# A fused fp32 model on one core: two homes for the scan's decay rows, another order inside a scan tile, and the weights' low parts written over their raw copies

## What is computed

```python
def hybrid_mixer(h, pos, w_in, conv_w, conv_b, ...):
    ...
    xs, b_in, c_in = split_cols(xbc, (SSD_INNER, SSD_GROUPS * SSD_STATE, SSD_GROUPS * SSD_STATE))
    ...
    dtf = jax.nn.softplus((dt_f + dt_bias_f).astype(jnp.float32)).reshape(b, s, SSD_GROUPS, SSD_HPG)
    ...
    y_fwd = ssd_chunked(xh, dtf, af, b_in, c_in)
    ...
    y = y_fwd + y_bwd + d_skip.reshape(SSD_GROUPS, SSD_HPG, 1).astype(xh.dtype) * xh
    y = gated_group_rmsnorm(y.reshape(b, s, SSD_INNER), z, ssd_norm_g)
    branch_ssd = y @ w_br_ssd
    ...
    return (g_ssd * branch_ssd + g_attn * branch_attn) @ w_out
```

## Time and profile before

| what | value |
|---|---|
| three runs | 2862.0, 2860.92, 2841.12 us |
| their median | 2860.92 us |
| the profiled execution | 2826.98 us |
| its span, first to last instruction | 2825.3 us |
| mean granted clock of PE | 0.982 |
| PE, DVE, ACT, POOL busy | 94%, 51%, 44%, 3% of the span |

### The profile page before, as it was taken

The page is one execution under the profiler, slowest core; times in us unless marked ns, Lnnn a source line. Parts: engine busy times, 40 slices in busy tenths (PEclk is TensorE's granted clock), DMA queues, the critical chain, the costliest instruction groups (busy, mean ns, idle before and its releaser), DMA issues.

```text
span 2825.3 us, 52535 instructions
## 1 busy us (share of the span) xinstructions
PE 2647.1 (94%) x20916; PEld 2429.6 (86%) x20916; DVE 1453.8 (51%) x2514; ACT 1244.8 (44%) x2045; POOL 83.5 (3%) x157
## 2 busy tenths in 40 slices
PE   7998999999998699999988999889988998999998
PEld 7985899999996399999987776679966986899998
DVE  3233476553424766664466777752376343433333
ACT  3335354432425644442355777752465234333321
POOL 0000000000000000000001211200000000000000
PEclk9999999999999999999999999999999999999999
DMA  6310122222321022223253454532211231222231
GB/s 181 123 67 0 45 90 89 95 98 99 112 97 53 1 75 99 95 98 119 98 187 117 169 197 156 186 123 98 89 46 53 97 105 45 75 97 97 97 105 68
DMA packets 74693, 278.20 MB, mean 98 GB/s; under 512 B 9642, under 2 KB 9674, under 8 KB 74048
## 3 DMA queue, kind: packets, MB, share of 16 engines
q1 hardware_dynamic: 60816, 217.42, 22.4%
q0 software_dynamic: 13744, 58.88, 6.8%
HBM read 267.03 MB, written 9.24 MB: 98 GB/s over the span
## 4 chain that ended last, share of the span: by engine, by line
PE 79%; DVE 9%; ACT 5%; DMA 4%; issue 3%; DVEq 0%; ACTq 0%; POOL 0%; POOLq 0%; SPq 0%
PE acc L338 66%; PE acc L369 2%; DMA res_tmp<-scratch_rows 2%; PE ps L813 1%; DMA w_raw<-in_stream 1%; PE ps L369 1%; PE acc L1467 1%; ACT w_hi L313 1%; PE ps L453 1%; DVE big L2173 1%; DVE big L1276 1%; PE ps L1740 1%; PE acc L827 1%; DVE res_tmp L1872 1%; DVE res_tmp L1358 1%
## 5 line engine op out<-in xcount | busy, mean ns | idle before, releaser
L338 PE MATMUL acc<-x_split,w_hi 128*128 128x256 f32 x7968 | 1254.6, 280 | 23.6 <-DVE x_split L1363 12.0
L338 PEld LDWEIGHTS acc<-x_split,w_hi 128*128 128x128 f32 x7968 | 1072.3, 190 | 28.6 <-issue 22.2
L319 DVE TENSOR_TENSOR w_lo<-w_raw,w_hi 128x1024 fp32r<-128x1024 f32 x405 | 493.1, 1222 | 605.9 <-ACT w_hi L313 605.9
L338 PE MATMUL acc<-x_split,w_lo 128*128 128x256 f32 x3984 | 786.3, 279 | 0.0
L313 ACT ACTIVATE w_hi<-w_raw 128x1024 fp32r<-128x1024 f32 x405 | 424.9, 1054 | 578.8 <-PE acc L338 527.2
L338 PEld LDWEIGHTS acc<-x_split,w_lo 128*128 128x128 f32 x3984 | 609.1, 190 | 0.0
L338 PE MATMUL acc<-big_r,w_hi 128*128 128x256 f32 x3560 | 559.0, 279 | 7.7 <-DVE big_r L2226 3.4
L338 PEld LDWEIGHTS acc<-big_r,w_hi 128*128 128x128 f32 x3560 | 477.5, 188 | 9.8 <-issue 3.6
L338 PE MATMUL acc<-big_r,w_lo 128*128 128x256 f32 x1780 | 351.7, 279 | 0.0
L338 PEld LDWEIGHTS acc<-big_r,w_lo 128*128 128x128 f32 x1780 | 271.6, 189 | 0.0
L1842 ACT ACTIVATE res_tmp<-res_tmp 128x512 f32<-128x512 f32 (+3 forms) x256 | 120.7, 550 | 43.4 <-DVE res_tmp L1867 42.9
(11 more groups left out here) (291 smaller groups left out, 2579.1 us busy)
## 6 DMA issues: line engine op xcount, KB each, us to landing
w_raw<-in_stream SPq DMA_DIRECT2D x405, 512.0 KB, 3.3
res_tmp<-scratch_rows POOLq DMA_DIRECT2D x128, 320.0 KB, 5.7
scratch_bias<-res_tmp POOLq DMA_DIRECT2D x1, 2560.0 KB, 55.3
res_tmp<-in_x SPq DMA_DIRECT2D x2, 1024.0 KB, 7.7
res_tmp<-scratch_bias POOLq DMA_DIRECT2D x8, 256.0 KB, 4.4
scratch_x<-res_tmp POOLq DMA_DIRECT2D x1, 2048.0 KB, 8.1
scratch_kv<-big POOLq DMA_DIRECT2D x1, 2048.0 KB, 8.7
res_tmp<-scratch_x POOLq DMA_DIRECT2D x1, 2048.0 KB, 8.5
```

What stands on the lines that cost most here:

```text
L319: dve.tensor_tensor(w_lo[:, u.slot], w_raw[:, u.slot], w_hi[:, u.slot].bitcast(F32), ALU.subtract).then_inc(lo_done, 1)
L338: mm = pe.matmul(a[:, h], w, AR[:, x + k, h], start=(k == 0 and w is wh and x == hi and h.start == 0), stop=(k == total - 1 and w is wl), ...
```

## The change

1. `w_raw` is placed at the address of `w_lo`; `split_lo` works in place. `load_unit` waits for `units_used` of unit u−4 in place of `lo_done`. This holds for all stages.
2. The space becomes 8 more slots in the arena: `RES` 64, `TMP` 72, 84 slots; slots of the scan are renumbered (`CB` 58, `TAB` 63, `ROWS` 64, `XT` 46, `XTOK` 56).
3. The decay rows have two homes, by the parity of f. POOL's loop has 8 turns of 16 DMAs (it had 16 of 8); a home's next rows are requested when PE has used that home, so one tile ahead.
4. Inside a feature tile x is multiplied before z, and ACT's and DVE's parts are in another order; the weight stream's order follows.
5. The first gate tile of br_ssd is multiplied ahead of `heads(15)` and the last `square_sum`.

```diff
-RES = 60
-TMP = 68
-N_SLOTS = 76
+RES = 64
+TMP = 72
+N_SLOTS = 84
...
-        w_raw = ctx.enter_context(nc.sbuf_tensor("w_raw", [P, RING, BLK * P], F32))
         w_hi = ctx.enter_context(nc.sbuf_tensor("w_hi", [P, RING, BLK * P], F32R))
+
+        home = nc.sbuf_base
         w_lo = ctx.enter_context(nc.sbuf_tensor("w_lo", [P, RING, BLK * P], F32R))
+        w_raw = nc.alloc_sbuf_tensor_at("w_raw", [P, RING, BLK * P], F32, offset=home)
...
-                sp.wait_ge(lo_done, (u + (-RING)).count + 1)
+                sp.wait_ge(units_used, (u + (-RING)).count + 1)
...
             def body(i):
-                for c in range(CH):
-                    for b in range(2):
-                        pool.wait_ge(ev("s_pv"), 8 * i + (2 * c + b + 1))
...
+                for p in range(2):
+                    for c in range(CH):
+                        for b in range(2):
+                            pool.wait_ge(ev("s_pv"), 16 * i + (8 * p + 2 * c + b + 1))
+                            src = SCR_ROWS[ds(4 * i + (2 * p + b), 1), BACK[c]:BACK[c] + S + P].to_broadcast([P, S + P])
+                            pool.dma_start(part(p, b, c), src).then_inc(ev(f"s_row_in{p}{c}"), 16)
+            repeat(pool, SSD_TILES // 2, body)
...
+
+            product_tile(pe, Units(UB["br_ssd"]), Tiles(TB["br_ssd"]), XH, XL)
             heads(SSD_TILES - 1, 3)
             square_sum(GROUPS - 1)
...
-                    conv5_act(act, tz + 1, 8 + f, x)
-                    act.activation(A.at(VH, f), acc[tz.bank][:], ACT.Silu).then_inc(acc_free[tz.bank], 1)
-                    split_hi(act, uz + RING)
-                    split_hi(act, uz + 1 + RING)
+                    conv5_act(act, tx, 8 + f, x)
+                    evacuated(act, tx)
+                    act.activation(x, x, ACT.Silu).then_inc(ev("s_xt"), 1)
+                    tile_done(act, ux + 1)
+                    act.activation(A.at(VH, f), acc[(tx + 1).bank][:], ACT.Silu).then_inc(acc_free[(tx + 1).bank], 1)
+                    split_hi(act, ux + RING)
                     if j == 0:
                         table_rest(g)
-                    evacuated(act, tz + 1)
-                    act.activation(x, x, ACT.Silu).then_inc(ev("s_xt"), 1)
...
                     for c in range(CH):
+                        if c == 2:
+                            act.wait_ge(ev("s_xtt"), f + 1)
+                            act.activation(A[:, XTOK + j % 2], ps[:, 2], ACT.Copy).then_inc(ev("s_xtok"), 1)
+                            split_hi(act, ux + 1 + RING)
...
-                    conv5_dve(dve, tz + 1, f + 8, f + 8, x)
+                    conv5_dve(dve, tx, f + 8, f + 8, A[:, XT + j % 2])
+                    cap(g, j, 0)
+                    cap(g, j, 1)
                     if j == 0:
                         table_diagonals(g)
-                    split_lo(dve, uz + RING)
-                    split_lo(dve, uz + 1 + RING)
+                    if j or not first:
+                        out(4 * g + (j - 1), (j - 1) % 4)
+                    split_lo(dve, ux + RING)
...
+                    cap(g, j, 2)
+                    times_cb(f, j, 0)
+                    cap(g, j, 3)
+                    times_cb(f, j, 1)
+                    split_lo(dve, ux + 1 + RING)
...
+                    times_cb(f, j, 2)
+                    times_cb(f, j, 3)
...
-                product_tile(pe, u, t, XH, XL)
+                if j or stage != "br_ssd":
+                    product_tile(pe, u, t, XH, XL)
...
-        unit_stack(interleave(z, xs, 1), (8,)),
+        unit_stack(interleave(xs, z, 1), (8,)),
```

More of the change, by code:

```diff
@@ L1564, in build, with rows_buf, part @@
         onward = const[:, CONST["onward"]:CONST["onward"] + P]
-        def rows_buf(b):
-            return A[:, ROWS + 5 * b:ROWS + 5 * b + 5].rearrange("p b n -> p (b n)")
-        def part(b, c):
-            return rows_buf(b)[:, BACK[c]:BACK[c] + S + P]
+        def rows_buf(p, b):
+            at = ROWS + 10 * p + 5 * b
+            return A[:, at:at + 5].rearrange("p b n -> p (b n)")
+        def part(p, b, c):
+            return rows_buf(p, b)[:, BACK[c]:BACK[c] + S + P]
         cb_packed = A[:, CB:CB + 5].rearrange("p b n -> p (b n)")
@@ L1624, in bcdt_act @@
             act.activation(d, d, ACT.Ln).then_inc(ev("s_logdt"), 1)
-            rows = rows_buf(0)
+            rows = rows_buf(0, 0)
             act.wait_ge(ev("s_rows"), 8)
@@ L1810, in group @@
                     f = 4 * g + j
-                    uz, tz = Units(UB["ssd"] + 2 * j, g, 8), Tiles(TB["ssd"] + 2 * j, g, 8)
+                    ux, tx = Units(UB["ssd"] + 2 * j, g, 8), Tiles(TB["ssd"] + 2 * j, g, 8)
                     if j == 1 and not first:
@@ L1853, in ssd_dve, with cap @@
             dve.wait_ge(ev("s_tab"), 2)
-            dve.memset(small[:, 41:42], 0.0).then_inc(ev("s_pv"), 2 * CH)
+            dve.memset(small[:, 41:42], 0.0).then_inc(ev("s_pv"), 4 * CH)
             dve.memset(small[:, 42:43], 0.0).then_inc(ev("s_w"), 1)
-            def cap(f, head, c):
-                for b in range(2):
-                    dve.wait_ge(ev(f"s_row_in{b}{c}"), 16 * (f + 1))
-                x = A[:, ROWS:ROWS + 10].rearrange("p (b m) n -> p b (m n)", b=2)
+            def cap(g, j, c):
+                p, head = j % 2, g * 8 + 2 * j
+                dve.wait_ge(ev(f"s_row_in{p}{c}"), 64 * g + 32 * (j // 2 + 1))
+                x = A[:, ROWS + 10 * p:ROWS + 10 * p + 10].rearrange("p (b m) n -> p b (m n)", b=2)
                 x = x[:, :, (S + 2 * P) * c:(S + 2 * P) * c + 2 * P].rearrange("p b (k n) -> p b k n", k=2)
@@ L1867, in cap, with times_cb @@
                 dve.tensor_tensor(x, x, own, ALU.min).then_inc(ev("s_cap"), 1)
-            def times_cb(f, b, c):
-                dve.wait_ge(ev("s_e"), 8 * f + (2 * c + b + 1))
-                w, cb = part(b, c), cb_packed[:, BACK[c]:BACK[c] + S + P]
-                dve.tensor_tensor(w, w, cb, ALU.mult).then_inc(ev("s_w"), 1)
+            def times_cb(f, j, c):
+                for b in range(2):
+                    dve.wait_ge(ev("s_e"), 8 * f + (2 * c + b + 1))
+                    w, cb = part(j % 2, b, c), cb_packed[:, BACK[c]:BACK[c] + S + P]
+                    dve.tensor_tensor(w, w, cb, ALU.mult).then_inc(ev("s_w"), 1)
             def out(f, j):
                 v = A.at(VL, f)
-                dve.wait_ge(ev("s_pv"), 8 * f + 4 * CH)
+                dve.wait_ge(ev("s_pv"), 8 * f + 6 * CH)
                 dve.wait_ge(ev("s_xt"), f + 1)
@@ L1909, in group @@
                     f = 4 * g + j
-                    uz, tz = Units(UB["ssd"] + 2 * j, g, 8), Tiles(TB["ssd"] + 2 * j, g, 8)
-                    x = A[:, XT + j % 2]
-                    conv5_dve(dve, tz + 1, f + 8, f + 8, x)
+                    ux, tx = Units(UB["ssd"] + 2 * j, g, 8), Tiles(TB["ssd"] + 2 * j, g, 8)
+                    conv5_dve(dve, tx, f + 8, f + 8, A[:, XT + j % 2])
+                    cap(g, j, 0)
+                    cap(g, j, 1)
                     if j == 0:
                         table_diagonals(g)
-                    split_lo(dve, uz + RING)
-                    split_lo(dve, uz + 1 + RING)
+                    if j or not first:
+                        out(4 * g + (j - 1), (j - 1) % 4)
+                    split_lo(dve, ux + RING)
                     if j == 2 and not first:
                         scaled(g + (-1))
-                    if j or not first:
-                        out(4 * g + (j - 1), (j - 1) % 4)
                     if j == 0:
@@ L1923, in group @@
                         dve.wait_ge(ev("s_cb_rest"), 4 * g + 4)
+                    cap(g, j, 2)
[3 more added lines that the diff above has]
+                    split_lo(dve, ux + 1 + RING)
                     if j == 3 and not first:
                         lows(g + (-1))
-                    for c in range(CH + 1):
-                        if c < CH:
-                            cap(f, g * 8 + 2 * j, c)
-                        if c:
-                            times_cb(f, 0, c - 1)
-                            times_cb(f, 1, c - 1)
+                    times_cb(f, j, 2)
+                    times_cb(f, j, 3)
             group(0, True)
@@ L1953, in gated_act @@
             if not first:
-                act.wait_ge(ev("s_pv"), 2 * CH * (SSD_TILES + 1))
+                act.wait_ge(ev("s_pv"), 2 * CH * (SSD_TILES + 2))
             per = 1 + len(blocks)
```

17 lines of the change are left out of this document (6 added, 11 removed).

## The result

The changed kernel took 2911.35 us (median of 4) beside 2851.02 before: ratio 1.0262, 95% interval 1.0212 to 1.0312 (the two medians alone stand at 1.021, 60 us apart; the ratio is taken from single runs set against each other, here and below). Forecast were 2917 us and 1.020 of the median shown. Repeated beside the experiments it stood at 1.021 (1.0156 to 1.0264) and 1.0293 (1.0251 to 1.0336). The profiled execution has a span of 2914.8 us against 2825.3, +89.5. That is more than the 60 of the medians because the execution profiled before, at 2826.98, was quicker than all four that were timed beside this one.

A forecast was written before the change was run, and what follows sets the result against it. PE, busy 94% of the span, was taken as the bound. Terms 69.7 − 8 − 5.4 = +56.3 on the profiled 2826.98 gave 2883; against the median, 34 higher, 2917 (+2.0%), range 2900 to 2935, 8 in 10 2872 to 2946.

The forecast's parts named there:

- The start: Loads beside the bias write land after 22.8 us and only four units are there, so PE waits: +19 us.
- Rival A: At the start a load beside the bias write lands after 9.2 us, costing 2, not 19; time 2900; chance 0.17.
- Borders, norms, tails: Late split_hi or split_lo delays work PE needs: four phase borders 11.6, two norms 6.8, five layer-norm tails 17.0 us.
- The memory's stage: Late loads at the memory's norms and keys, its end and two smaller places: together +11.3 us (6 to 14).
- The clock: Some four PE waits become longer than 3.4 us and bring the lower clock behind them: +4 us (0 to 10).
- Steady stages: In steady product stages ACT idles 3 to 4 us between evacuations, so the later loads cost nothing there.
- Rival D: In up and ffn_in, loads over 3.9 us stall each pair of tiles: +20 to +30, time 2942; chance 0.17.
- The scan: Rows requested a tile earlier and the new order gain 2 us a group of four feature tiles: −8 us.
- a sign of being wrong: The forecast is wrong if a feature tile in the scan takes 18 us; 19.9 to 20.4 was expected.
- rival B: The scan becomes bound by PE, −39 in place of −8, and the start costs half; time 2876; chance 0.15.
- The gate tile: br_ssd's first gate tile fills PE's 8.38 us wait for the last weights at the scan's end: −5.4 us.
- The other sign of being wrong: The forecast is wrong if PE's idle time outside the scan grows by less than 40 us.

The follow-up runs named there:

- e1: The kernel before, raw copies in their own home, with only each load's wait changed from lo_done to units_used of unit u−4; ratio 1.0323.
- e11: The changed kernel with the bias row in slots 60 and 61 and its write to DRAM issued only when even_in's 28 units are used; ratio 1.0164.
- e8: The kernel before, with only loads of units 40–79, 140–179 and 344–379 (steady parts of up0, up1, ffn_in) waiting for units_used; ratio 1.0065.
- e3: The changed kernel, but outside bcdt and ssd raw copies have eight arena slots of their own and their loads wait for lo_done; ratio 0.9979.
- e7: e3 with one edit: in the first feature tile DVE cuts the diagonals ahead of the first two caps; ratio 0.9921, 2811.3 us.
- e2: The kernel before with only the first gate tile of br_ssd multiplied ahead of heads(15); ratio 1.0001.
- e9: e7 without the gate tile ahead of heads(15), which stands behind square_sum again; ratio 0.9965.
- c0: The kernel before, unchanged, run beside the other experiments and profiled on their chip; ratio 0.9989.
- e5: The changed kernel, unchanged, on the chip of the experiments; ratio 1.021.
- e10: The changed kernel, unchanged, run again beside e11 on one chip; ratio 1.0293.

## Why the prediction was right

The sign held, the cost outside the scan came by the mechanism that was named (e1), and the time was 2911.35 where 2917 was forecast. So close a hit is luck in part. The working started from the profiled execution and added 56.3 us; between the profiles it was 89.5, and the forecast of 2883 us for that execution was 33 short. Of the 89.5 some 19 are pace, which no term had, and about 70 are left. The 34 us that were added to get to the median made up for it: the execution profiled before was unusually quick, the one profiled after was not. Terms were off both ways:

- **The start, +19**: 21.6 us of waits against 1.76, and 5.5 more of clock behind them. e11 shows the write as cause. Rival A's 9.2 us for a load are refuted: the first one beside the write took 23.3 us (35.05 to 58.41) with no other load under way for the first 5 of them. The packets of 35 to 38 us and then of 50 to 70, in the changed kernel (q0 is the write, q1 the loads):

```profile
q1 hardware_dynamic: 64, 0.25, 28.5%
...
q0 software_dynamic: 190, 0.97, 41.1%
q1 hardware_dynamic: 191, 0.72, 8.7%
```

Half of the load moved in its first 3 us and the rest came much later. The rule of the Trainium skill named in the prediction (DMA: Bandwidth & Descriptors, Queues, rings and completion order: turns between queues, packet by packet) is in the trace once three loads are under way, 190 packets beside 191, and the loads then land 7.5 us apart. It does not give the time of the first load; the row did. What holds its second half back is open.
- **Borders, norms, tails: 11.6 + 6.8 + 17.0**: measured 18, 7 and 16. The waits shown rose by somewhat less than forecast (1.07 to 2.27 with 1.26 a little earlier, 2.5 for 2.9; 0.87 to 3.50, 2.6 for 3.4), but PE then runs for some us at the lower clock.
- **The memory's stage, 11.3**: measured 12.6; the wait at its end rose from 3.37 to 6.46, 3.1 for 3.3.
- **The clock, +4 for four places, was mis-sized.** The mean granted clock is 0.964 against 0.982: at two levels that is 210 us at the lower one against 102 us. If all the 42 us more of idle time lie in the 108 more, PE worked at half the rate for 66 (e8: 20 matmuls in 4 us at the lower level, 38 at the upper), which is 33 us in place of 4, an estimate; it and the pace make up the 47.6 of longer busy time. Shorter waits than the 3.4 of the prediction do it too: 2.27 behind 1.26 at the retention, with a clock of 0.85 at 212 to 222 us.
- **Steady stages, 0**: PE's idle time in up0 and up1 grew by 2 to 3 us at their starts; e8 says 8 us or more for all. The term should have been 5 to 10, an estimate. Rival D's stalls a pair did not come: in all of up0's products PE idles 2.2 us in the changed kernel, in up1's 2.7.
- **The scan, −8**: −26.0 up to the last transposes, and +5.9 at its first tile, −20 in all. The step that failed took 8.0 us for a load's landing. It is 3.4, and not because the rows are asked for a tile ahead: e1, whose rows are not, has 3.3 with the short wait alone. The prediction counted that wait as a pure loss in the scan too, where it is the larger part of the gain. With 3.4 both `split_hi` waits were near nothing and a tile took 18.6 us in the mean (1640.0 to 1918.9 for 15; 20.3 before). That is outside the 19.9 to 20.4 forecast and close to the 18 given as a sign of being wrong; rival B was nearer for the steady tiles, though not for its −39. What the prediction had not seen is the first tile, where caps that wait for rows stand ahead of the diagonals (e3, e7).
- **The gate tile, −5.4**: the wait went from 8.38 to 1.31, and 3.71 came back at a later piece of heads(15), since ACT's last exps are later in the new order. e2 and e9 show 4 to 6 us in their traces; no time resolves it.

The other sign of being wrong did not come: PE's idle time outside the scan grew by 59 us (42 in all, 17 less between 1527 and 2075 of before), where under 40 would have spoken against the forecast.

The change's own parts, from the experiments: the short ring is +3.2% (e1), with some 110 us lost outside the scan and 18 gained in it by the traces. The rest of the change takes off 0.3 to 1.1% (e1 against 1.021 to 1.029), on different chips; in the traces PE idles 6 to 8 us less than in e1 (218.7 against 210.7 to 212.8), which is 0.3%.

## What to carry to other kernels

A buffer that is freed for one stage and shortens a prefetch for all stages is paid for at every place where the prefetch is looked at: the start, each phase border, each norm. Count these places, one latency each and the lower clock behind them, before you count the gain; or, as e7 does, lend the space only to the stage that needs it. Test a change's cheapest part alone in every stage: here the later load, paid for everywhere else, made the scan quicker by itself. In an in-order engine, put what waits for a transfer behind what others wait for, and look at the first iteration on its own.

## What was not expected of the hardware

**Two paces at one clock.** With a granted clock of 1.00 and PE never idle, 20 us of up1 hold 179 matmuls in one execution and 172 in another. c0 and then e9:

```profile
1130.00:1150.00 20.00, 20.00 (x179) 20.00 (x178) 11.88 (x19) 7.98 (x11) 0.00 (x0) 1.00 0.32 100
```

```profile
1130.00:1150.00 20.00, 20.00 (x172) 20.00 (x172) 11.02 (x18) 8.45 (x12) 0.00 (x0) 1.00 0.31 105
```

The pace changes where stages meet and holds through a stage: 0.113 or 0.118 us from one matmul's start to the next. ffn_in and ffn_out are at the first in the profiles of before, c0, e8 and e7, at the second in e2 and e9. One kernel has both: the changed one has 179 matmuls at 2600 to 2620 us in its first profile and 172 in e5 and e10, and at 1250 to 1270 it is 172, 179 and 172. A full change of these two stages is 14 us, 0.5%. Which one a stage gets was not found. A single profile's step of some us in a product stage says nothing for that reason, and e3's trace (−22 in the scan's part) and its time (−6) can differ by it.

**A short wait is enough.** 3.06 us of PE's idle time at the start of up1 (e8) went with a window of clock 0.83; the same work in c0, 0.07 us not busy, had 1.00. The first is e8, the second c0:

```profile
1060.00:1080.00 20.00, 16.94 (x125) 16.75 (x124) 15.02 (x24) 10.36 (x14) 0.00 (x0) 0.83 0.24 79
```

```profile
1066.00:1086.00 20.00, 19.93 (x176) 19.74 (x175) 15.32 (x23) 11.37 (x15) 0.00 (x0) 1.00 0.40 132
```
